# The opening loads of a two-block transformer kernel, reordered: constants, parameters, memory and two weight slots behind x

## The reference

```python
h = x @ w_in                                   # 1024 -> 384 + 256 + 64
c_q = _rmsnorm(h[..., :MLA_Q_RANK], g_q)
c_kv = _rmsnorm(h[..., MLA_Q_RANK:MLA_Q_RANK + MLA_KV_RANK], g_kv)
k_r = _rope(h[..., MLA_Q_RANK + MLA_KV_RANK:], pos)
...
bias = rel_bias[_t5_bucket(dist)].astype(jnp.float32)     # of the second layer's attention
...
kv = rms_norm(mem, mem_g) @ w_kv                          # of the second block's memory branch
```

## Time and profile before

| | |
|---|---|
| median of 3 runs | 1120.15 us (1117.88 to 1120.17) |
| profiled execution | 1118.81 us |
| span of its instructions | 1117.0 us |
| granted TensorE clock, mean | 0.995 |
| busy: PE, PEld, DVE, ACT, POOL | 97%, 88%, 68%, 58%, 1% |
| HBM read | 179.74 MB, 162 GB/s over the span |

### The profile page before, as it was taken

The page is one execution under the profiler, slowest core; times in us unless marked ns, Lnnn a source line. Parts: engine busy times, 40 slices in busy tenths (PEclk is TensorE's granted clock), DMA queues, the critical chain, the costliest instruction groups (busy, mean ns, idle before and its releaser), DMA issues.

```text
span 1117.0 us, 22415 instructions
## 1 busy us (share of the span) xinstructions
PE 1083.2 (97%) x8339; PEld 979.8 (88%) x8339; DVE 760.6 (68%) x1300; ACT 645.0 (58%) x1148; POOL 10.0 (1%) x25
## 2 busy tenths in 40 slices
PE   6999999999999899999989999999989999999998
PEld 5978999999887689999989988898889989999997
DVE  5877655557876675555786775636774868877776
ACT  5877555544676765544468753434566447666663
POOL 1000000000000000000000000000000000000000
PEclk9999999999999999999999999999999999999999
DMA  9636656555564356656555332212235664665662
GB/s 348 192 136 208 207 181 185 184 186 188 176 215 135 95 173 186 187 188 188 187 171 169 133 115 77 69 48 77 76 114 170 190 188 124 202 189 184 183 192 94
DMA packets 49170, 181.76 MB, mean 163 GB/s; under 512 B 5536, under 2 KB 5696, under 8 KB 48208
## 3 DMA queue, kind: packets, MB, share of 16 engines
q1 hardware_dynamic: 46512, 168.32, 47.5%
q0 software_dynamic: 1584, 7.63, 2.2%
q10 hardware_dynamic: 1008, 4.89, 1.2%
HBM read 179.74 MB, written 1.07 MB: 162 GB/s over the span
## 4 chain that ended last, share of the span: by engine, by line
PE 85%; DVE 7%; ACT 5%; DMA 2%; issue 1%; DVEq 0%; ACTq 0%; SPq 0%
PE acc L706 27%; PE work L669 12%; PE work L673 12%; PE work L672 12%; PE acc L669 3%; PE acc L672 3%; PE acc L673 3%; ACT whi L1407 1%; DVE wlo L1982 1%; PE work L786 1%; PE work L1167 1%; PE work L1146 1%; DVE res L2005 1%; DMA sqr<-x_t 1%; DMA raw<-weights 1%
## 5 line engine op out<-in xcount | busy, mean ns | idle before, releaser
L1982 DVE TENSOR_TENSOR wlo<-raw,whi 128x1024 fp32r<-128x1024 f32 x319 | 389.0, 1223 | 170.4 <-ACT whi L1407 169.2
L1407 ACT ACTIVATE whi<-raw 128x1024 fp32r<-128x1024 f32 x319 | 335.7, 1056 | 129.1 <-PE acc L706 84.9
L669 PE MATMUL work<-xh,whi 128*128 128x256 f32 x1104 | 314.1, 284 | 5.1 <-DVE xl L1992 4.0
L672 PE MATMUL work<-xl,whi 128*128 128x256 f32 x1104 | 311.6, 282 | 0.0
L673 PE MATMUL work<-xh,wlo 128*128 128x256 f32 x1104 | 311.4, 282 | 0.0
L669 PEld LDWEIGHTS work<-xh,whi 128*128 128x128 f32 x1104 | 209.5, 190 | 14.7 <-issue 4.9
L672 PEld LDWEIGHTS work<-xl,whi 128*128 128x128 f32 x1104 | 209.1, 189 | 3.5
L673 PEld LDWEIGHTS work<-xh,wlo 128*128 128x128 f32 x1104 | 209.8, 190 | 0.0
L706 PE MATMUL acc<-whi,hl 128*128 128x512 f32 x344 | 108.0, 395 | 0.0
L706 PE MATMUL acc<-wlo,hh 128*128 128x512 f32 x344 | 108.0, 395 | 0.0
L706 PE MATMUL acc<-whi,hh 128*128 128x512 f32 x344 | 108.0, 395 | 0.0
(11 more groups left out here) (443 smaller groups left out, 1569.9 us busy)
## 6 DMA issues: line engine op xcount, KB each, us to landing
raw<-weights SPq DMA_DIRECT2D x319, 512.0 KB, 3.6
gb<-ln_rows POOLq DMA_DIRECT2D x4, 1024.0 KB, 6.6
memraw<-mem_t ACTq DMA_DIRECT2D x1, 1024.0 KB, 15.1
x<-mem_tok ACTq DMA_DIRECT2D x1, 1024.0 KB, 18.2
x<-x_tok ACTq DMA_DIRECT2D x1, 1024.0 KB, 8.5
qlat<-bias_scratch POOLq DMA_DIRECT2D x1, 1024.0 KB, 10.7
qlat<-bias_scratch POOLq DMA_DIRECT2D x4, 256.0 KB, 4.4
out_tok<-res SPq DMA_DIRECT2D x4, 256.0 KB, 2.1
```

Of the source, the lines that this page charges most:

```text
L669: a = mm(dst, whi[:, n % RING, col], hi, start=start, stop=False, skip_group_check=shared)
L672: mm(dst, whi[:, n % RING, col], lo, start=False, stop=False, skip_group_check=shared)
L1407: act_fn(whi[:, n % RING, :], raw[:, n % RING, :], ACT.Copy).then_inc(cut_hi, 1)
L1982: tt(wlo[:, n % RING, :], raw[:, n % RING, :], whi[:, n % RING, :].bitcast(F32), ALU.subtract).then_inc(cut_lo, 1)
```

## The change

Four loads (constants, parameters, the two copies of memory) go from ScalarE's queue to Pool's, behind a wait for `x_rest_loaded`, and ahead of the store of the bias rows. SP waits for the same semaphore before it loads slot 2, and with it everything behind. PE starts with 16 products of zeros (128 x 128 against 512 columns, bfloat16) into the first bank, then chunk 0, then the bias table's product, then chunk 1. VectorE drains `brow` in turn 1 of the loop, behind the cut of slot 4, and waits for the constants in turn 2. The three small operations on `par` go to the place right before `layer_norm("ln0")`. The wait for `zeros_set` moves from the first layer norm to PE's start.

```diff
 _results("in", [0])
 _results("brow", [0])
-_results("in", range(3))
+_results("in", range(1, 3))
...
             for n in range(RING):
+                if n == 2:
+                    sp.wait_ge(sig("x_rest_loaded"), 16)
                 sp.dma_start(raw[:, n, :], w[n]).then_inc(raw_loaded[n], 16)
...
             pool.dma_start(bandt, band_in).then_inc(sig("band_loaded"), 16)
+            pool.wait_ge(sig("x_rest_loaded"), 16)
+            first_con = CCOL["blockones"]
+            pool.dma_start(con[:, 0:first_con], consts_in[:, 0:first_con]).then_inc(sig("con_loaded"), 16)
+            pool.dma_start(par[:, :], params_in).then_inc(sig("par_loaded"), 16)
+            pool.dma_start(memraw[:, :, :], memt).then_inc(sig("mem_loaded"), 16)
+            pool.dma_start(x[:, :, :], mem_tok).then_inc(sig("mem_tok_loaded"), 16)
             wait_drained(pool, ("brow", 0))
...
-            pe.wait_ge(sig("band_loaded"), 32)
-            close_result(mm(open_result(("brow", 0))[0:16, 0:384], relb[:, :], bandt[:, 0, :], start=True, stop=True), ("brow", 0))
+            pe.wait_ge(sig("zeros_set"), 1)
+            zero_products(open_result(("in", 0)), 16)
             for j in range(3):
                 chunk("in", j, ("in", j), xh, xl, (lambda k: pe.wait_ge(sig("x_cut"), k // 2 + 1)) if j == 0 else None)
+                if j == 0:
+                    pe.wait_ge(sig("band_loaded"), 32)
+                    close_result(mm(open_result(("brow", 0))[0:16, 0:384], relb[:, :], bandt[:, 0, :], start=True, stop=True), ("brow", 0))
...
-            act.dma_start(con[:, 0:first_con], consts_in[:, 0:first_con]).then_inc(sig("con_loaded"), 16)
-            act.dma_start(par[:, :], params_in).then_inc(sig("par_loaded"), 16)
-            act.dma_start(memraw[:, :, :], memt).then_inc(sig("mem_loaded"), 16)
-            act.dma_start(x[:, :, :], mem_tok).then_inc(sig("mem_tok_loaded"), 16)
...
             for j in range(6):
                 if j != 4:
                     cuts("in", j)
+                if j == 1:
+                    bank = wait_filled(dve, ("brow", 0))
+                    dve.wait_ge(sig("band_loaded"), 32)
+                    drain(stt(brow, bank[0:16, 0:384], SWA_D ** 0.5, bandt[0:16, 1, :], ALU.mult, ALU.add), ("brow", 0))
+                if j == 2:
+                    dve.wait_ge(sig("con_loaded"), 16)
...
+            dve.wait_ge(sig("par_loaded"), 16)
+            ts(keep[:, :], par[:, PCOL["mu"]:PCOL["mu"] + 14], -1.0, 1.0, ALU.mult, ALU.add)
+            ts(less_k_a[:, :], par[:, PCOL["k_a"]:PCOL["k_a"] + 4], -1.0, None, ALU.mult)
+            own.link(ts(nsink[:, :], par[:, PCOL["sinks"]:PCOL["sinks"] + 16], -1.0, None, ALU.mult))
             dve.wait_ge(sig("x_tok_loaded"), 16)
             layer_norm("ln0", "wo", "ln_mix_g", "ln_mix_b", 0, lambda: cuts("memva", 0))
```

More of the change, by code:

```diff
@@ L204, in _results @@
     RESULTS.extend((stage, n) for n in names)
+_results("in", [0])
 _results("brow", [0])
-_results("in", range(3))
+_results("in", range(1, 3))
 _results("kvstat", [0])
@@ L945, in _ @@
             token_major("memva", 2, T, memh, meml)
-            pe.wait_ge(sig("zeros_set"), 1)
             feature_major("ln0")
@@ L1447, in _ @@
             act.dma_start(sqr[:, 2:DC, :], xt[:, 2:DC, :]).then_inc(sig("x_rest_loaded"), 16)
-            first_con = CCOL["blockones"]
-            act.dma_start(con[:, 0:first_con], consts_in[:, 0:first_con]).then_inc(sig("con_loaded"), 16)
-            act.dma_start(par[:, :], params_in).then_inc(sig("par_loaded"), 16)
-            act.dma_start(memraw[:, :, :], memt).then_inc(sig("mem_loaded"), 16)
-            act.dma_start(x[:, :, :], mem_tok).then_inc(sig("mem_tok_loaded"), 16)
             def root_table():
@@ L2085, in _ @@
                 cut(n)
[L2086 to L2093, removed]
             def turned(dst, bank, buffers, ready, n, width, key):
```

## The result

Kernel after: 1121.41 us, the median of 15 runs (1119.08 to 1123.52); before, beside it on the same chip, 1119.71 (15 runs). The ratio is 1.0022 with a 95% interval of 1.0012 to 1.0032: the change costs 1.3 to 3.6 us, 2.5 by the ratio and 1.7 by the medians. Its profiled execution took 1120.10 us (span 1118.3) where that of before took 1118.81 (1117.0). The prediction said 1120.5, 0.35 above before: the range (1117.0 to 1123.2) holds the time, but the change is a loss, at 0.22% about as large as the 0.2% that it called no change, and larger than its sum by 1.3 us (medians) to 2.1 (ratio).

A forecast was written before the change was run, and what follows sets the result against it. The opening was taken as bound by DMA bytes, slot 5 last, delaying PE's latent work at 31.71. Terms 0 + 0.35 on 1120.15 gave 1120.5 us (chance 0.47), range 1117.0 to 1123.2.

The forecast's parts named there:

- x's rest: Opening load of x's larger part: lands at 10.49, gain between 0 and 0.8 us, taken as 0.
- The hole: DMA engines nearly idle around 11 us behind the new waits; weights flow from 12.8, Pool's loads from 14.4.
- Slots 4 and 5: Opening weight loads: slot 4 at 18.2, slot 5 at 21.5 or 20.9 against 22.14 before.
- 0 for the shift of 31.71: PE's first product on the latent, at 31.71 before, was taken not to move: 0 us.
- slot 5 before 20 or after 23: Landing times in us of weight slot 5 in the opening, named as a sign that the prediction was wrong.
- both outer rivals: The faster rival, 1118.2 or 1117.4 us, chance 0.25, and the slower rival, 1122.9 us, chance 0.20.
- The slower rival: Opening loads: Pool's flow together with the weights, the hole is passed on, slot 5 at 24.6; +2.4 + 0.35, 1122.9 us; chance 0.20.
- Zeros and clock: PE's start: zeros take 3.6 to 6.4 us, over by 7.5; chunk 0 ends at 13.8 or 15.5; no chunk on the chain.
- the case that the chain is right: PE's early chunks are not on the chain of waits, so zeros and clock gain nothing; opposite rival 1119.0 us, chance 0.08.
- the faster rival: Opening loads: Pool's queue starts slowly, weights run ahead, slot 5 at 18.1; -2.3 + 0.35, 1118.2 us; chance 0.25.
- Bias product, drain, store: Bias rows' work moved later in the opening: drain done at 20.9, store about 27 against 32 wanted; costs nothing.
- Small operations: Three VectorE operations on the parameters, now between last cut and residual near 98.63: +0.35 us, for certain.

The follow-up runs named there:

- e2: Changed kernel with the four loads back on ScalarE's queue at the start, SP's wait kept; one execution, 1121.73 us.
- e1: Changed kernel without SP's wait before slot 2; 1121.22 us, ratio 1.0021 to the kernel before.
- e3: Changed kernel with memory's two loads held on Pool's queue until slot 4 is cut; 1120.25 us, ratio 1.0012 to the kernel before.
- e4: Changed kernel with 26 products of zeros in place of 16; 1121.89 us, ratio 1.0032 to the kernel before.
- e8: Kernel before with 16 products of zeros ahead of the bias product, nothing else; 1119.20 us, ratio 1.0004.
- e5: Changed kernel with the three small operations moved to turn 2 of the loop, ahead of slot 5's cut; 1121.04 us, ratio 1.0023 to the kernel before.
- e10: Changed kernel once more, unchanged; 1121.25 us, ratio 1.0020 to the kernel before.
- e6: Kernel before with memory's two copies on Pool's queue, behind the bias rows' store and slot 4's cut; 1118.64 us, ratio 1.0003.
- e9: Changed kernel with all loads but memory at the start, memory behind slot 4's cut, 26 products of zeros plus 8 in chunk 0, small operations early; 1118.01 us, ratio 0.9995.

## Why the prediction was nearly right, step by step

**What bounds.** Right for before and after. The chain of after is that of the earlier trace rows with every link in its place, and each thing that made slot 5 early made the first product early until PE itself was the bound.

**x's rest.** Predicted 10.49 with a gain of 0 to 0.8 and a reason that the neighbour slot stays; it came at 9.91. In e2, with the loads on its own queue, 9.93: no gain by moving them, as predicted. But slots 2 and 3, now held back, had been neighbours too, and the kernels with SP's wait have x 0.5 us sooner. The term was put at nothing and measured about 0.5, inside its range.

**The hole.** Right: 2.2 us were to pass between a load's issue and its bytes, and between 9.4 and 11.6 the engines stood nearly idle. Taking off x's 0.58, slot 2 was due at 13.5 (came 13.46), slot 3 at 15.7 (15.63), constants at 16.4 (16.49). Pool's constants took 6.3 us from issue to landing for 512.5 KB, SP's slot 2, alone at first, 3.5. The DMA issues of after:

```profile
memraw<-mem_t POOLq DMA_DIRECT2D x1, 1024.0 KB, 9.6
x<-mem_tok POOLq DMA_DIRECT2D x1, 1024.0 KB, 12.9
con<-table POOLq DMA_DIRECT2D x1, 512.5 KB, 6.3
par<-params POOLq DMA_DIRECT2D x1, 165.5 KB, 6.7
```

**Slots 4 and 5: the step that failed.** The prediction gave the weights three quarters of the engines beside the parameters, for 1.6 us, "slot 4 at 18.2, and 0.12 MB of slot 5", so that 0.40 MB were left to fetch beside memory. Slot 4 came at 19.86, and when memory's rows began 0.90 MB of the two slots were left. The view of the queues tells why: constants and parameters together took 2.7 us of flow (0.68 MB), not the 4.2 of the sum, and in these the weights got 0.45 MB, not 1.03. The three quarters came from the earlier trace rows, where the parameters went on ScalarE's queue, in rows of 1.3 KB (165.5 KB over 128 partitions). On Pool's queue there are no such packets: 54 under 2 KB up to 16.2, all of them under 512 B, where the earlier trace rows has 292, 148 of them under 512 B. They passed in larger ones, and memory's long rows began at 16.2, where the sum, less x's 0.58, had 18.0. Up to there the sum had held: at 16.4 slot 4 was to have 0.14 MB, and at 16.2 the weights had 1.19 MB, 0.14 MB of them of slot 4. What failed is the 1.6 us beside the parameters, with 0.51 MB for the weights: it did not exist. The rate beside memory was right: 0.90 MB in 6.5 us is 138 GB/s, the lower of the two ends (138 and 177). So slot 5 was due at 20.3 to 20.9 with x's 0.58 taken off, and came at 23.63; and "0 for the shift of 31.71" had to be +1.56. That meets a sign that the prediction itself had named for being wrong, "slot 5 before 20 or after 23". The time lies in the range all the same, which had been drawn wide enough for both outer rivals; x's early landing, put at nothing, took 0.58 off the delay. That part is luck.

**The slower rival** had the mechanism: the hole is passed on, slot 5 at 24.6, +2.4. It measured +1.5 at the slot, 0.58 of the difference being x's early landing and 0.4 the size. Its condition, that the constants land within about 2 us of slot 2, did not hold (16.49 and 13.46). e1 and e3 point to another one: what of slots 4 and 5 is not yet in when memory's rows begin. With slot 4 in before them (e1, 13.6) slot 5 came at 21.57, with both in before them (e3) at 18.87. The rival had 0.20 against the forecast's 0.47, and its mechanism is nearer to what happened; the time lies nearer to the forecast.

The Trainium skill (DMA: Bandwidth & Descriptors, Queues, rings and completion order) says that an engine goes round its queues packet by packet. The trace agrees in the counts: beside memory's 8 KB rows, 251 packets of Pool against 237 of SP in 6.5 us, and bytes of 1.84 to 0.90 MB. A packet of these loads is one row here.

**Zeros and clock.** 16 products took 5.94 us (3.6 to 6.4) and were over by 6.94 (7.5). Chunk 0 ended at 15.3, at the lower clock (15.5), after the clock had risen at 5.7 and fallen at 9.1, behind PE's wait from 6.94. Nothing came of it, as predicted for the case that the chain is right; e4 and e8 confirm it. But PE's own chunks were slower than in the sum: chunk 2 ended at 22.2, not near 20.0 (before 21.6), with chunk 0 at half clock and the bias product behind it. PE waited only 1.62 us for the latent, so the early slot 5 of the faster rival would have been worth no more than that, unless the clock stayed up as in e3.

**Bias product, drain, store.** The product went at 15.47, the drain at 22.12 and the store landed at 28.7, ahead of the 32 when it is wanted; lora and gate were issued at 29.0 and 29.6, behind it, and landed at 31.9 and 32.6. Costed at nothing, and none is on the chain.

**Small operations.** Predicted +0.35: behind the cut 1.49 against 1.14 us, +0.35 exactly; to the residual 0.45.

**The sum.** 1.56 + 0.45 is the residual's +2.01 (100.64 against 98.63). Of this +1.3 was left at the end of the profiled span; both had three late stretches, and the rest is the scatter of the table. At equal late clock, after's six runs at 0.991 (four late stretches and the fall at the start) have a mean of 1121.35, before's at 0.994 (four late stretches too; the record of its clock begins at 14.9 and has no fall at the start) one of 1119.72 beside e5 to e8: +1.6. But after's seven runs at 0.992 have a mean of 1121.82, above those at 0.991, and its profiled execution, 1120.10, is the lowest of them; in e8 the runs at 0.992 are not above those at 0.991 (1119.48 and 1119.78). So the usual execution of after loses more than its profile shows. What that is stays open. One candidate: e4 and e5 fell to half clock behind PE's wait for the latent (3.3 and 1.7 us) and lost 1.5 us more by it. The profiles of after and e10 (waits of 1.62 and 1.74) don't show that, so for the usual run of after it stays possible, not shown. The prediction had priced a stretch of half clock at 1.7 us; it cost about 1.1.

## What to carry to other kernels

A wait for one load's completion ahead of others leaves the DMA engines empty for the time from issue to first bytes, here 2.2 us, against 0.5 that it gained for the load waited for. Before adding one, find which transfer the chain waits for, how many of its bytes are left when the next bulk load begins, and what rate it has beside that load (here 138 GB/s of 421 beside 8 KB rows). To speed up a needed transfer, delay the bulk load that shares the engines with it (e3, e6: slot 5 came 4.3 to 4.8 us earlier), not everything. Then see what bounds next: in e6 PE's own chunks did, and left 1.18 us of the 4.3 at the residual and nothing that the medians could show. And small work that moves out of an early place with slack must not land behind the last cut ahead of a residual: 0.45 us.

## What was not expected of the hardware

- Two queues shared by packets, not bytes: 138 GB/s for the weights' 4 KB rows beside memory's 8 KB rows. The parameters' rows of 1.3 KB travelled in larger packets from Pool's queue than from ScalarE's: 32 packets in after's trace, 128 in that of before.
- Products of zeros lifted the clock at 5.7 us, but it fell again at 9.1, in the midst of chunk 0's first pair, behind a wait of 2.09 us, and stayed at half until 16.0. The same 16 products lifted it at 3.9 us in e5 and at 6.4 in e3, and in e3 it did not fall behind a wait of 1.63. With 26 zeros and chunk 0's pause filled by 8 more (e9) it stayed up.
- Late stretches of 3.4 us at half clock come or don't, one to four in an execution, about 1.1 us each. For a gain of 1 to 2 us of 1119 this is the noise to beat; the split at a fixed product, or runs of equal mean clock, showed more than the medians did.
